# Reordering the opening of the first block of a two-block model on one core of a Trainium2 chip

## The reference, cut to what matters

```python
def first_block(x, c, w_ada, b_ada, g_norm, w_in, ...):
    mod = c @ w_ada[l] + b_ada[l]
    shift, scl, gate = jnp.split(mod, 3, axis=-1)
    h = rms_norm(x, g_norm[l]) * (1.0 + scl[:, None, :]) + shift[:, None, :]
    proj = h @ w_in[l]
    u_pool, z_pool, q, k, v, z_attn, m_pool, m_attn = jnp.split(proj, splits, axis=-1)
    ...
    q = partial_rope(q...); k = partial_rope(k...)
    y_attn = moba_attention(q, k, v) * jax.nn.silu(z_attn)
    ...
    x = x + gate[:, None, :] * (merged @ w_out[l])
    return rms_norm(x, g_final)

def second_block(x, c, w_ada, ...):
    mod = jax.nn.silu(c) @ w_ada[l] + b_ada[l]      # "second condition" c_2
    ...                                              # retention, sparse attention, then the PEER layer
```

## Time and profile before

| | us |
|---|---|
| median of 3 runs (1314.39 to 1316.32) | 1314.98 |
| the profiled execution, whole | 1316.01 |
| its span (first to last record) | 1314.2 |
| TensorE busy (94% of the span) | 1240.6 |
| VectorE busy (65%) | 858.4 |
| ScalarE busy (43%) | 564.3 |
| GpSimd busy (32%) | 419.8 |

### The profile page before, as it was taken

The page is one execution under the profiler, slowest core; times in us unless marked ns, Lnnn a source line. Parts: engine busy times, 40 slices in busy tenths (PEclk is TensorE's granted clock), DMA queues, the critical chain, the costliest instruction groups (busy, mean ns, idle before and its releaser), DMA issues.

```text
span 1314.2 us, 18368 instructions
## 1 busy us (share of the span) xinstructions
PE 1240.6 (94%) x6978; PEld 1020.0 (78%) x6978; DVE 858.4 (65%) x1818; ACT 564.3 (43%) x1027; POOL 419.8 (32%) x231
## 2 busy tenths in 40 slices
PE   5789999899999789999999999999999999999996
PEld 2668875355455559999999999999988888888885
DVE  5568754444533553499966899899766666656666
ACT  1545421102123323444446665555455554545553
POOL 0767810000000000388887777776600000000000
PEclk9889999998989789999999999999999999999999
DMA  9968763436313033255554445555466666656564
GB/s 378 373 256 332 308 256 138 172 131 256 128 64 128 1 128 129 67 189 180 185 184 156 158 159 156 159 161 149 157 201 207 227 227 204 205 187 194 195 195 152
DMA packets 54519, 244.23 MB, mean 186 GB/s; under 512 B 6944, under 2 KB 7328, under 8 KB 42016
## 3 DMA queue, kind: packets, MB, share of 16 engines
q1 hardware_dynamic: 54000, 242.34, 52.8%
q10 hardware_dynamic: 432, 0.72, 0.2%
HBM read 240.94 MB, written 2.10 MB: 185 GB/s over the span
## 4 chain that ended last, share of the span: by engine, by line
PE 90%; DVE 6%; issue 1%; ACT 1%; DMA 1%; SPq 0%; POOL 0%; POOLq 0%; DVEq 0%
PE bank L1353 9%; PE bank L1350 9%; PE bank L1349 9%; PE bank L992 7%; PE banks L992 6%; PE banks L1389 4%; PE bank L1395 4%; PE banks L1392 4%; PE bank L1389 4%; PE banks L1395 4%; PE bank L1392 4%; PE banks L1363 3%; PE bank L1040 2%; PE bank L1044 2%; PE bank L1048 2%
## 5 line engine op out<-in xcount | busy, mean ns | idle before, releaser
L699 POOL TENSOR_TENSOR split_r<-ring,split_r 128x1024 fp32r<-128x1024 f32 x128 | 307.7, 2404 | 160.1 <-ACT split_r L912 160.0
L912 ACT ACTIVATE split_r<-ring 128x1024 fp32r<-128x1024 f32 x256 | 269.1, 1052 | 180.4 <-PE bank L1353 180.4
L1349 PE MATMUL bank<-h_high_r,split_r 128*128 128x256 f32 x1024 | 251.2, 283 | 1.7 <-ACT split_r L912 1.7
L1350 PE MATMUL bank<-h_low_r,split_r 128*128 128x256 f32 x1024 | 251.1, 283 | 0.0
L1915 DVE TENSOR_TENSOR split_r<-ring,split_r 128x1024 fp32r<-128x1024 f32 x128 | 156.8, 1225 | 65.6 <-ACT split_r L912 65.6
L1349 PEld LDWEIGHTS bank<-h_high_r,split_r 128*128 128x128 f32 x1024 | 196.2, 192 | 1.9 <-issue 1.9
L1350 PEld LDWEIGHTS bank<-h_low_r,split_r 128*128 128x128 f32 x1024 | 196.3, 192 | 0.0
L1353 PE MATMUL bank<-h_high_r,split_r 128*128 128x256 f32 x1024 | 143.7, 283 | 0.2 <-POOL split_r L699 0.2
L1353 PEld LDWEIGHTS bank<-h_high_r,split_r 128*128 128x128 f32 x1024 | 132.1, 192 | 0.4 <-POOL split_r L699 0.4
L966 ACT ACTIVATE gs_r<-G 128x256 fp32r<-128x256 f32 x128 | 53.5, 418 | 172.6 <-PE bank L1395 172.6
L703 POOL TENSOR_TENSOR small<-small 128x1 f32<-128x1 f32 x2 | 1.5, 758 | 359.1 <-DVE small L1941 359.1
(11 more groups left out here) (377 smaller groups left out, 2081.6 us busy)
## 6 DMA issues: line engine op xcount, KB each, us to landing
ring<-in_down SPq DMA_DIRECT2D x128, 512.0 KB, 3.5
ring<-in_up SPq DMA_DIRECT2D x128, 512.0 KB, 3.5
G<-in_ada SPq DMA_DIRECT2D x32, 1024.0 KB, 10.3
G<-in_in SPq DMA_DIRECT2D x32, 1024.0 KB, 7.2
G<-in_out SPq DMA_DIRECT2D x8, 1024.0 KB, 8.3
G<-in_wq SPq DMA_DIRECT2D x8, 1024.0 KB, 6.0
tab<-in_ada SPq DMA_DIRECT2D x4, 1024.0 KB, 5.6
G<-in_poolup SPq DMA_DIRECT2D x2, 1024.0 KB, 6.0
```

Of the source, the lines that this page charges most:

```text
L699: pool.tensor_tensor(wsplit[:, j % SPLIT, 1, :], raw[:, j % RAW, :], wsplit[:, j % SPLIT, 0, :].bitcast(F32), ALU.subtract).then_inc(low_r ...
L912: nc.scalar.activation(wsplit[:, n % SPLIT, 0, :], raw[:, n % RAW, :], ACT.Copy).then_inc(high_ready, 1)
L1349: mm(o, w[0][:, c, :], h_high[:, c, :], start=(c == 0), stop=False)
L1350: mm(o, w[0][:, c, :], h_low[:, c, :], start=False, stop=False)
```

## The change

Three things move, and one place changes. ScalarE scales its own banks ahead of the first high copy, instead of waiting for VectorE's bank first, and copies both token blocks of a half together. The two instructions of `sc2` move on VectorE from ahead of the scaling to behind the second subtraction. The steps `qkT` move from between panels 3 and 4 to behind panel 4 and its `ada` step. Since `qk_nat` (columns 2048 to 4096 of the scratch region) is then still in use when the first unit of panel 5 is rounded, that unit's place goes from 2048 to 12288.

```diff
--- before.py
+++ after.py
@@ -156,8 +156,8 @@
     high("in1", 2, (1,))
     panel("in1", 2)
     panel("in1", 3)
+    panel("in1", 4)
     out.extend(("qkT", qk, t) for qk in range(2) for t in range(NT))
-    panel("in1", 4)
     later = [[("panel", *p)] for p in IN1_LATER]
     later[6] = [("poolT", 0), ("poolT", 1)] + later[6]
     later += [[("pool", 0), ("pool", 1)], [("upT", 0), ("upT", 1), ("up", "poolup", 0, 0), ("up", "poolup", 0, 1)]]
@@ -230,10 +230,8 @@
 
 
 
-HIGH_AT = [("hT3", 0), ("G", 14336), ("G", 7168), ("hT3", 0), ("G", 14336), ("G", 7168),
-           ("G", 2048), ("hT3", 0), ("G", 14336), ("G", 2048), ("hT3", 0), ("G", 14336),
-           ("G", 2048), ("hT3", 0), ("G", 14336), ("G", 2048), ("hT3", 0), ("G", 14336),
-           ("G", 2048), ("hT3", 0)]
+HIGH_AT = [("hT3", 0), ("G", 14336), ("G", 7168), ("hT3", 0), ("G", 14336), ("G", 7168), ("G", 12288)]
+HIGH_AT += [(("hT3", 0), ("G", 14336), ("G", 2048))[k % 3] for k in range(13)]
 SPLIT_ROWS = [("ring", 5632), ("G", 0)]
 POOL_UNITS = [k for k, (n, _) in enumerate(UNITS) if STREAM[n][0] == "in1"]
 DVE_UNITS = [k for k in range(len(UNITS)) if k not in POOL_UNITS]
@@ -772,13 +770,10 @@
                                                    bias=modB[:, blk_n, cc:cc + 1])
                     bank_free(ins, s)
                     if blk_n == 0:
-                        x0_high_part(1, half)
-                        if half == 0:
-                            x0_high_part(0, 1)
+                        for q in range(NT):
+                            x0_high_part(q, half)
                     if blk_n == 2:
                         high_part(1, half)
-                elif s == ("xT", 0, 0, 0):
-                    x0_high_part(0, 0)
                 elif kind == "xT" and s[1] == 2:
                     high_part(0, s[3])
                 elif kind == "high":
@@ -1587,9 +1582,6 @@
             dve.wait_ge(start_cols, 3)
             link(tt(modB[:, 0, 4:8], ps[6][:, 0:4], b1c[:, 4:8], ALU.add))
             dve.sem_inc(mod_ready, 1)
-            dve.wait_ge(c2_exp, 1)
-            link(ts(sc2, sc2, 1.0, 0.5, ALU.add, ALU.mult))
-            link(tt(sc2, sc2, c2, ALU.mult))
 
             for s in STEPS:
                 kind = s[0]
@@ -1615,6 +1607,9 @@
                             evacuated(dve, ("xT", 0, t, half))
                         c = slice(4 * half, 4 * half + 4)
                         tt(x0_low[:, c, :], hT[0][:, c, :], x0_high[:, c, :].bitcast(F32), ALU.subtract).then_inc(x0_low_ready, 1)
+                    dve.wait_ge(c2_exp, 1)
+                    link(ts(sc2, sc2, 1.0, 0.5, ALU.add, ALU.mult))
+                    link(tt(sc2, sc2, c2, ALU.mult))
                 elif kind == "proj" and s[1] == "in1" and s[2] in (2, 3):
                     _, _, i, t = s
                     dst = qk_nat[:, i - 2, t, :].rearrange("p (h e) -> p h e", h=H)
```

## The result

The changed kernel takes 1309.09 us (median of 6 runs, 1307.66 to 1311.56) against 1315.33 (6 runs, 1314.36 to 1316.67) for the kernel before, timed beside it: ratio 0.9949, 95% interval 0.9939 to 0.9959. Six more runs in a later comparison had 1309.32. Over all comparisons the median of before is 1315.9 (68 runs; one more, of 2714.2 us, is left out) and that of after 1309.3 (12 runs): 6.6 us less, where the sum forecast 8.05. The profiled execution took 1307.66 us with a span of 1305.7; before it was 1316.01.

A forecast was written before the change was run, and what follows sets the result against it. TensorE was taken to bound the kernel, with 90% of the last chain. Terms -3.25 - 6.1 - 1.4 + 2.7 = -8.05 us took 1316.01 to 1307.96, set to 1307.0 for the median; range 1304.5 to 1310.8.

The forecast's parts named there:

- the sum: All terms up to panel 5's start: -3.25 - 6.1 - 1.4 + 2.7 = -8.05 us, panel 5 at about 78.75.
- The opening: Ahead of the first product: ScalarE and VectorE stop waiting, first product at 38.36 instead of 41.61, gain 3.25 us.
- The wait ahead of panel 4: Between panels 3 and 4: TensorE waits only for bank 1, 7.58 us becomes 1.5, gain 6.1.
- Rival C: Ahead of panel 4: VectorE frees bank 1 sooner, no wait at all, 1.5 us more gained, 1305.5; chance 0.09.
- The clock in panel 4: Panel 4 runs at full clock after the shorter wait, 11.0 us instead of 12.40, gain 1.4.
- Rival A: Clock falls in the 1.5 us wait ahead of panel 4, its 1.4 us not gained: 1308.4; chance 0.12.
- The bare turning: Behind panel 4: the moved transposes and their last copy lie uncovered ahead of the score, cost 2.7 us.
- rival D: ScalarE caught behind panel 5's load, delaying panel 4's evictions; 1317.6 if the load takes 20.3 us; chance 0.04.
- E: Nothing changes, because a later wait on a load takes the gain back: 1315; chance 0.05.
- B: Opening's gain given back because panel 4's load and GpSimd's chain don't move: 3.25 us less, 1310.2; chance 0.08.
- the shift should reach the end: Behind panel 5: engine orders unchanged and panels asked for earlier, so the whole 8.05 us gain should last.
- the correction by 1.03 us: Profiled execution lay 1.03 us over the median of three, so 1307.96 was lowered to 1307.0.

The follow-up runs named there:

- after_again: The changed kernel run again with nothing altered, for a second profile: 1309.32 us, ratio 0.9943 to the kernel before.
- hold: The changed kernel plus eight and four unread products ahead of the pooled branch's two groups of transposes: 1310.49 us, ratio 0.9956 to the kernel before.
- turning_only: The kernel before with only the moved qkT steps and the new place for a unit, opening unchanged: 1313.33 us, ratio 0.9976.
- late_acc: The changed kernel with VectorE's accumulation for the ada step behind both token blocks of panel 2: 1311.10 us, ratio 0.9957 to the kernel before.
- opening_only: The kernel before with only the new order of ScalarE's and VectorE's work in the opening: 1311.84 us, ratio 0.9967.
- sc2_only: The kernel before with only the two sc2 steps moved on VectorE: 1314.85 us, ratio 0.9993.
- scalar_only: The kernel before with only ScalarE's order changed: 1315.03 us, ratio 0.9988.

## Why the prediction was right, and where its sum was off

**The opening, -3.25:** measured from the rounding, -3.16; the two single steps alone give 2.03 and 1.48 at the first product, as the working had it from one engine's wait for the other. The copy did not wait longer by the scaling side by side: VectorE's first bank still takes half of 2.64 us. That `sc2` is hidden in its new place holds (0.34 us, and panel 2's first result comes later). What the step missed is the level. It let panel 2 keep the 12.5 us that it had; in the profile of after panel 2 took 13.90 (36.96 to 50.86) with the granted clock at 0.50 in this window of after:
```profile
33.00:43.00 10.00, 6.91 (x19) 5.56 (x19) 5.58 (x13) 8.16 (x15) 7.87 (x6) 0.50 1.01 413
```
The line that ends panel 2 there:
```profile
50.86 1.98 PE L1035 MATMUL banks<-G_r,ring_r 128*128 128x512 f32 x8
```
In after_again panel 2 took 12.41 us, and in `hold`, whose products start at 37.08, 12.31, so this costs between nothing and 1.4, and an early start alone does not decide it. What does isn't settled.

**The wait ahead of panel 4, 7.58 to 1.5:** 1.25 in one profile of after (6.33 gained), 0.34 from panel 3's end in the other, within the bounds of 4.9 to 7.6. Rival C was not a rival but the other face of the same term: which of VectorE's two operations meets a GpSimd instruction differs between executions of one kernel. The Trainium skill (SBUF — State Buffer, "SBUF: two separate sides") calls it a lock for a whole instruction; the rows agree, 1.32 and 1.41 us beside GpSimd and 0.23 where the operation fell into a gap.

**The clock in panel 4, -1.4:** 11.01 us from first product to the `ada` step (62.99 to 74.00) and 11.01 in after_again, forecast 11.0. Rival A's fall was in neither, nor after the 1.38 us wait of `turning_only`. The number was right, but its support was weak. It leaned on a later stretch with TensorE nearly idle at 1.00. That stretch lies 101 us behind panel 5, in the very wait in which six other profiles show the clock falling.

**The bare turning, +2.7:** from the `ada` step to panel 5 it takes 4.53 us (74.00 to 78.53) and took 1.80 before: +2.73. VectorE's `ada` result was over at 75.75, ahead of the transposes at 76.17, so the half microsecond of spare time was just enough; `late_acc` shows the case in which it is not. ScalarE had panel 5 rounded at 71.6, before the first eviction at 73.29: rival D did not come, nor E. (D's 17.7 us are counted from 61.7, where 69.5 - 7.2 gives 62.3; nothing else hangs on it.) Nor did B. GpSimd's low parts of panel 4, two units of four instructions, were over at 66.08, and TensorE wanted the second at 72.18:
```profile
56.04 10.04 POOL L677 TENSOR_TENSOR wq_low_r<-G,G_r 128x512 fp32r<-128x512 f32 x8
...
72.18 1.98 PE L1043 MATMUL bank<-wq_low_r,ring_r 128*128 128x512 f32 x8
```

**The sum:** 78.75 was forecast for panel 5, and the profiles of after have 78.53 and 77.63. That the first is so near is in part luck, the 1.49 us of the earlier rounding. Counted from the rounding, its steps are -3.16 (opening) + 1.39 (panel 2) - 6.33 (wait) - 1.39 (clock in panel 4) + 2.73 (turning) = -6.76: the mechanisms were the right ones, and the term that the sum put at nothing, the level in panel 2, took 1.4 us. In after_again panel 2 lost nothing and the wait was shorter, -9.25 in all, but "the shift should reach the end" failed: the stretch behind panel 5 took 1229.7 us, 2.3 more than before (1227.4; 1227.2 in the first profile of after). A stage beyond 87 us that is longer than it was is a sign of being wrong that the prediction had named.

The third mis-sized step is the correction by 1.03 us to the median of three runs: over 68 runs the median of before is 1315.9, so the profiled 1316.01 had been typical, and the forecast of 1307.96 made from it needed no lowering. Of the 2.3 us between 1307.0 and 1309.3, the correction accounts for about 1, and what is left, 1.3 us, is of the size of the loss in panel 2 in one profile and of that behind panel 5 in the other. Which of them the unprofiled runs had is argued from these profiles and not shown; `hold`, which was to show the second, moved the loss elsewhere.

Where the clock falls in an execution, and whether it falls more often in after than in before, is open. The spreads point that way: 67 of the 68 runs of before lie between 1314.1 and 1317.7 us (the other took 1325.4), the twelve of after between 1305.3 and 1311.6. The start of the rounding adds to the spread of every kernel.

## What to carry to other kernels

Move work that waits behind a panel that doesn't, and check whose buffers both need: here 7.6 us of waiting became 0.3 to 1.3 in the two profiles of the changed kernel, for 2.7 us of transposes laid bare, of which a short product put behind them won back 0.8. Where two engines each wait for the other's list, take both steps: alone they brought the first product 2.0 and 1.5 us forward, but only 0.3 and 0.7 us were left at panel 5, against 3.8 for both. A gain read in one pair of profiles is good to about the scatter of the stretches that no edit touches, here 31.4 to 33.0 us ahead of the change and 1227.2 to 1229.7 behind it for one and the same kernel. Count from the last event ahead of the change, and take a second profile before a step is called right or wrong for 2 us.

## What the runs showed of the hardware that had not been expected

- The same instructions with the same waits, TensorE busy for 8.01 of 10 us, ran once with a granted clock of 1.00 and once with a mean of 0.83. The Trainium skill (TensorE: Matmul & The Clock Gate, "Part 1: The HAM clock gate (the "warmup" mystery)") says that what the gate looks at is not tied to the kernel's start, so that the number of slow products varies from run to run. The trace agrees: panel 2 of the changed kernel took 13.90 us in one execution and 12.41 in the other. It adds that the level differs between executions in the middle of a kernel, too, where the stretch behind panel 5 took 1227.2 to 1233.2 us.
- Where unread products kept TensorE busy in the wait at +100 us, the clock stayed at 1.00 there in all four profiles, against four of the ten without them. In `hold` that shortened nothing. Ahead of the first products they did: the first eight took 2.08 or 2.09 us in the three profiles with them and 3.37 to 3.75 in the eleven without.
- GpSimd's four instructions for the first unit took 5.94 us in after and 4.93 before, where the earlier subtraction of VectorE (36.80, 1.36 us) now runs into them; it is 5.94 in `opening_only` as well, and 4.94 and 4.93 in `sc2_only` and `scalar_only`, whose subtraction starts when the last of the four is nearly through or over. The price fell on an engine with time to spare.
